# Moving one modulation block into attention, four products from GpSimd to VectorE, and a part of attention's modulation sums ahead of the gate products

## The chip, the cores and the metric

The kernel is one program on one core of a Trainium2 chip. The metric is the device time of one execution in microseconds (us). The engines are named as the profile names them: PE is TensorE's matmul, PEld its weight load, DVE is VectorE, ACT is ScalarE, POOL is GpSimd, SP is SyncE, whose queue issues the weight loads from HBM. Everything is float32.

## The reference

Two transformer blocks follow each other on 512 tokens of width 1024. What matters here, shortened:

```
mod = silu(c) @ w_ada + b_ada                    # 6 x 1024 numbers: shift, scale, gate of two branches
x = x + gate * rms_norm(mixer(rms_norm(x) * (1 + scale) + shift))      # mixer: two kinds of attention
x = x + gate * rms_norm(swiglu(...))
# second block: 9 x 1024 numbers from silu(c_2) @ w_mod_2 for x, and once more for 256 context tokens
x, xc = ffn with ffn_w_in_2[0], ffn_w_out_2[0]   # on x and on the context xc
x = x + gate * rms_norm(mLSTM and pooling mixer)
x = x + gate * rms_norm(swiglu(..., ffn_w_in_2[1], ffn_w_out_2[1]))
swiglu(h) = (silu(h @ w_gate) * (h @ w_up)) @ w_down        # 1024 -> 2816 -> 1024
```

## The kernel before

**Stages.** The first mixer (projections, selection, `attention`), then one block of code for the out-projection and two feed-forward layers (`stage_ffn_1_2`), the second mixer, and the last feed-forward layer.

**Attention** (line 1631) runs 48 pair steps; a step is a block of 128 queries with two heads. PE computes the scores of step i (L1706), turns the probabilities of step i - 2 (L1717) and multiplies those of step i - 3 with the values (L1734). Between them it takes 9, later 6 to 8 products of a `stream`: the feed-forward layer of the context tokens, which has nothing to do with attention. Its up part has tiles of 8 gate products (L874, bank 6) and 8 up products (L886, bank 7) up to step 23, its down part 8 outputs of 22 products (L913) from step 24 on. On DVE a step is two maxima (L1774), the normalisation of the step before (L1782, L1784 or L1788), and then `context_gate` (L952: waits for ACT's tanh of a finished gate tile, multiplies, frees bank 6) and `context_hidden` (L960, frees bank 7) of the tiles that fall due, and after them `some` instructions of modulation sums.

**Modulation.** The numbers of `mod` come in blocks of 512: a block's weights (2 MB, as two halves of 1 MB in `mod_half`) are multiplied by a vector and summed on DVE, eight sums (L1685, then seven L1687), a transpose (L699) and a reduction (L706), twice that with two vectors (for x and the context, blocks "mod" below 10). PE turns the result into columns with a small matmul (L776). `MODS_LATE` lists the jobs done in attention in order and `LATE_ENDS` the pair step by which each is due: a job begins in the step where the one before is due, and its instructions are spread evenly over its steps. Job j may begin when PE has turned job j - 2. The turning is placed at fixed tiles of the up part for jobs 0 to 5, ahead of down outputs 1, 3, 4, 5, 6 and 7 for jobs 6 to 11 (`more`), and at the end for 12 and 13. SP issues the half loads by `late(j, half)` (L1858), which waits until DVE has used up that half of the job before; between them stand the loads of the ring (L291), a ring of three buffers for all other weights, each of which waits until PE has left the buffer. `K.ring.load_ahead(sp, ("out1", 0))` loads half of w_out, 2 MB in three parts.

**The out-projection** (`out_tensor`, `out_scalar`, `out_vector`, lines 2150 to 2260) has 16 pieces of 8 products (L2144), for two halves of the tokens. ACT squares each piece (L1976) and scales it (L1977), DVE adds the squares (`y_add`, L1988), and after piece 8 PE sums them over the partitions (`y_sum`, L1997 and L1998). PE needs the addition of piece 6 and the square of piece 7 for it. Between the additions DVE does the update of the context tokens, coefficients, and two modulation blocks, 12 and 13 (`MODS_OUT`), whose ten instructions each (`side_sums`, L3088, seven of L3091, L3100, L3104) are taken by `spare(4)`, `spare(4)`, `spare(2)`, `spare(5)`, `spare(3)` and `spare(2)`. `spare(5)` stands after `coefs_2` and before the addition of piece 6. Their weights are loaded by `side_loads_out`.

**The three feed-forward layers** (calls 0, 1, 2 of `fast_tensor`, `fast_gpsimd`, `fast_scalar`, `fast_vector`) multiply in blocks with seven products in place of eight: POOL forms sums of weight blocks (four L2898 to L2903 for an up tile, L2911 and L2913, then L2973 and L2977, for a down output), DVE forms sums of token blocks and adds up the results. The up part has 22 tiles: four by themselves, then 8 pairs in a form of their own (`pair_tensor`, L2414), then two more by themselves (u = 4 = LEAD and u = 5). The products of a tile are named by lines: L2717, L2767, L2773, L2781, L2725, L2791, L2796; L2767 waits for POOL's L2900. A pair ends on POOL with `pair_products`: two products of Silu and up (L2662, 128x512 each) and a subtraction (L2666). A single tile ends there with L2945, L2947 and L2950. DVE makes `xs`, sums of the hidden blocks, for the down part: five L3074 after the last pair, L3261 for the tile u = 4, and L3209 for the last. The down part begins with L2839 (22 products with block b11), then L2847, which needs all of `xs`. In DVE's stream of a tile, L3166, L3233 and L3218 read the first results, L3267 gives block 21 and L3282 block 12, which ACT turns by Silu (L3040); ACT's L3038 is the Silu of block 11. In call 1 PE has 16 more products (L2806, the context's norm) ahead of L2839.

Of the kernel before, what the change touches and what calls it, by code (L numbers as in the profile page):

```python
# [9 lines left out]
ALU = mybir.AluOpType  # L10
# [72 lines left out]
def column_order():  # L83
# [5 lines left out]
    def plain(name):  # L89
# [16 lines left out]
HALF = SEQ // 2  # L106
MODS_START = 4
MODS_FIRST = 6
MODS_LATE = (("ada", 6), ("mod", 6), ("ada", 7), ("mod", 7), ("ada", 8), ("mod", 8), ("ada", 4), ("mod", 9), ("ada", 9),
             ("mod", 10), ("ada", 10), ("mod", 11), ("ada", 11), ("ada", 5))  # L110
LATE_ENDS = (4, 8, 11, 16, 18, 23, 27, 33, 36, 39, 41, 44, 46, 48)
MODS_OUT = (12, 13)
MODS_DOWN = {0: (14, 15), 1: (16, 17), 2: ()}
MODS_BOTH = 10
# [1516 lines left out]
def attention(K, M):  # L1631
# [64 lines left out]
    with nc.Block() as block:  # L1696

        @block.tensor
        def _(pe):
# [36 lines left out]
                last.then_inc(pv, 1)  # L1736

            columns = {f: {part: MODS_LATE[j]} for j, (f, part) in enumerate(((11, 0), (14, 1), (15, 0), (18, 1), (19, 0), (21, 1)))}
            more = {d: MODS_LATE[6 + j] for j, d in enumerate((1, 3, 4, 5, 6, 7))}
            stream = itertools.chain(  # L1740
                itertools.chain.from_iterable(context_up(
                    K, X, pe, f, columns.get(f, ()), (1,) if f == CTX_SCORER else (0, 1)) for f in ups),
# [15 lines left out]
                if i >= 3:  # L1758
                    values(i - 3)
            pe.wait_ge(X.y, KT)  # L1760
            modulation_columns(K, pe, MODS_LATE[12])
            modulation_columns(K, pe, MODS_LATE[13])

        @block.vector
        def _(dve):
# [26 lines left out]
            for i in range(len(pairs) + 1):  # L1792
                for half in range(2):
                    if i < len(pairs):
                        maximum(i, half)
                for half in range(2):
                    if i >= 1:
                        normalise(i - 1, half)
                for f in due(gate_slot, i):
                    context_gate(K, X, dve, f)  # L1800
                for f in due(up_slot, i):
                    context_hidden(K, X, dve, f)
                if i == LATE_ENDS[job] and job + 1 < len(MODS_LATE):
                    job += 1
                    left, steps = late_length(job), late_steps(dve, job)
                some = -(-left // max(LATE_ENDS[job] - i, 1))
                left -= some
                for _ in itertools.islice(steps, some):
                    pass

        @block.scalar
# [38 lines left out]
        def _(sp):  # L1850
# [32 lines left out]
            late(7, 1)  # L1883
            K.ring.load_ahead(sp, ("ctx_down", 3))
            late(8, 0)
            K.ring.load_ahead(sp, ("ctx_down", 4))
            late(8, 1)
            late(9, 0)
            K.ring.load_ahead(sp, ("ctx_down", 5))
            late(9, 1)  # L1890
            late(10, 0)
            K.ring.load_ahead(sp, ("ctx_down", 6))
            late(10, 1)
            late(11, 0)
            late(11, 1)
            K.ring.load_ahead(sp, ("ctx_down", 7))
            late(12, 0)
            late(12, 1)
            K.ring.load_ahead(sp, ("out1", 0))
            late(13, 0)  # L1900
            late(13, 1)
            K.ring.load_ahead(sp)
            sp.wait_ge(X.down, KT)
            sp.dma_start(K.x[:, :, CTX:TOK], K.spill).then_inc(K.restored, 16)
# [216 lines left out]
def out_fields(K, name, call, W, gain, scale, shift, banks, begun=0, context=False):  # L2121

    O = out_products(Fields(), name, banks, begun)
    O.context = context
    O.mm = Tally(K.out_mm, call * len(OUT_PIECES))
    flat = W.hid[:, :, :, :].rearrange("p a f n -> p (a f n)")
    y = flat[:, 0:KT * SEQ].rearrange("p (k n) -> p k n", k=KT)
    O.T = Tail(K, lambda k0, k1, a, b: y[:, k0:k1, a:b], OUT_PIECES, gain, W.squares, scale, shift,
               left=(2, 6))
    if context:  # L2130
        O.sq, O.sums, O.log, O.rstd_done, O.scaled, O.done = (K.sem(f"po_{n}") for n in (
            "sq", "sums", "log", "rstd", "scaled", "coefs"))
        O.total, O.rstd = K.ps[4][:, 0:CTX], W.side[:, 0:CTX]
        side_fields(K, O, W, MODS_OUT, 0)
        O.squares, O.z = ([W.side[:, CTX * i:CTX * i + CTX] for i in at] for at in ((1, 2), (3, 4)))
    return O

# [12 lines left out]
def out_tensor(K, O, pe):  # L2150

    for i in range(len(OUT_PIECES)):
        if i >= 3:
            O.T.s["scaled"].wait(pe, i - 2)
        out_piece(K, O, pe, i, range(4) if i < O.begun else range(KT), True).then_inc(O.mm.sem, 1)
        if i in (KT + 3, 2 * KT - 1):
            K.ring.left(O.mm.sem, O.mm.base + i + 1)
        if O.context and i < 4:
            for k in (2 * i, 2 * i + 1):
                pe.wait_ge(O.sq, k + 1)  # L2160
                pe.matmul(O.total, K.ones[:, :], O.squares[k % 2], start=(k == 0),
                          stop=(k == KT - 1)).then_inc(O.sums, 1)
        if O.context and i in (KT + 2, KT + 6):
            modulation_columns(K, pe, ("mod", O.side[0 if i == KT + 2 else 1]))
        if i == KT:
            y_sum(K, O.T, pe, 0)
        if i == KT + 4:
            x_sum(K, O.T, pe, 0)
# [133 lines left out]
def fast_fields(K, call, W, prev, gain, scale=None, shift=None, context=False, by_rows=None):  # L2302
# [13 lines left out]
    F.side = MODS_DOWN[call]  # L2316
    F.coefs = K.sem(f"coefs{call}") if F.side else None
    if F.side:
        side_fields(K, F, W, F.side, len(MODS_OUT) + sum(len(MODS_DOWN[c]) for c in range(call)))
    F.in_down = False  # L2320
    F.T = Tail(K, lambda k0, k1, a, b: K.h[:, k0:k1, CTX + a:CTX + b], FFN_PIECES, gain, W.squares, scale, shift,
               left=(2, 2) if context else (6, 6))
# [36 lines left out]
def pair_fields(K, F, scr, base):  # L2359
# [2 lines left out]
    counts = (96, 96, 96, 96, 96, 96, 48, 32) + (24, 24, 27, 1) + (8, 4, 4, 4, 8, 8)  # L2362
    n = len(F.pairs)
    done = dict(args=13, t=3 * n, s=3 * n, d1=n, d2=n, begun=2 * n, y_kept=2 * n, w=3 * n, f=3 * n, c=2 * n, full=n, rows=3 * n,
                diff=3 * n, cols=6 * n, silu=2 * n, hid=n, token=4, formed=n)
    F.R = {name: Tally(sem, count + done[name] * K.pair_calls) for name, sem, count in zip(PAIR_SEMS, spent, counts)}
    K.pair_calls += 1
    W = F.W
# [288 lines left out]
def pair_products(K, F, pool, e):  # L2657

    R, f = F.R, 2 * F.pairs[e]
    for n, (half, buf) in enumerate(((1, F.c_buf[e % 2]), (0, F.F_buf[e % 2]))):  # L2660
        R["silu"].wait(pool, 2 * e + n + 1)
        ins = pool.tensor_tensor(pair_hidden(F, e, half), buf[:, 0:2], buf[:, 2:4], ALU.mult)  # L2662
        if n == 0 and f + 1 >= FH:
            K.pool.link(pool, ins)
            j0, j1 = max(f, FH) - FH, f + 2 - FH
            pool.tensor_tensor(F.b12[:, j0:j1], F.b22[:, j0:j1], F.b12[:, j0:j1], ALU.subtract)  # L2666
    ins.then_inc(R["hid"].sem, 1)

# [30 lines left out]
def fast_tensor(K, F, pe):  # L2701
# [110 lines left out]
    for d in range(4):  # L2812
# [18 lines left out]

        if d == 0 and F.pairs:
            F.R["hid"].wait(pe, len(F.pairs))
            S["hid"].wait(pe, LEAD)
        else:
            S["hid"].wait(pe, FH if d == 0 else F.ups)
# [49 lines left out]
def fast_gpsimd(K, F, pool):  # L2886
# [47 lines left out]
        F.R["d2"].wait(pool, n)  # L2934
        up_weight_sums(LEAD + 1)

    for u, f in enumerate(F.tiles):
        j = f % FH
        one, two = (F.b11, F.b12) if f < FH else (F.b21, F.b22)
        if F.pairs and u == LEAD - 1:  # L2940
# [190 lines left out]
def side_loads_out(K, O, sp):  # L3131

    side_load(K, O, sp, 0, 0)
    side_load(K, O, sp, 0, 1)
    sp.wait_ge(*O.side_half[0])
    side_load(K, O, sp, 1, 0)
    sp.wait_ge(*O.side_full[0])
    side_load(K, O, sp, 1, 1)


def side_loads(K, F, sp):
# [27 lines left out]
def fast_vector(K, F, dve):  # L3169
# [19 lines left out]
    for u in range(F.units):  # L3189
# [50 lines left out]
        if u < F.units - 1:  # L3240
            give_22()
        if F.pairs and u == LEAD:
            F.R["hid"].wait(dve, len(F.pairs))
            steps = pair_hidden_sums(F, dve)
        if F.pairs and u == LEAD - 1:
            pair_rows(K, F, dve, 0, (0, 1))
# [19 lines left out]
        S["c21"].wait(dve, u + 1)  # L3266
        dve.tensor_tensor(out21, pc, F.v, ALU.add).then_inc(S["got21"].sem, 1)  # L3267
        spare(2)
        if F.ups <= u < F.units - 1:
            S["xsum"].wait(dve, x_count(d) + 4)  # L3270
            for a, b in HALVES:
# [8 lines left out]
            pair_rows(K, F, dve, 0, (2,))  # L3280
        S["c12"].wait(dve, u + 1)
        dve.tensor_tensor(out12, pb, F.v, ALU.add).then_inc(S["got12"].sem, 1)  # L3282
        spare(2)


# [852 lines left out]
```

## Time and profile before

| what | us |
|---|---|
| median of 3 runs | 2096.37 |
| the runs | 2096.37, 2096.44, 2093.59 |
| the profiled execution | 2093.89 |
| its span, first to last instruction | 2092.0 |
| PE busy | 2060.4 (98%) |
| DVE busy | 1509.1 (72%) |
| POOL busy | 837.2 (40%) |
| ACT busy | 535.2 (26%) |

The views are of that one profiled execution. Busy PE is not PE at its peak, since matmuls are pipelined and their ends are modelled. Times in the timelines are from the start of the span.

### The profile page before, as it was taken

The numbers are of one execution on the slowest core, as the hardware profiler recorded it, in microseconds if no ns is written. First come the engines' busy times: TensorE is split into PE (matmuls) and PEld (weight loads), VectorE is DVE, ScalarE is ACT, GpSimd is POOL, SyncE is SP. The second block draws the span as 40 slices with busy tenths as digits, with TensorE's granted clock in tenths as the row PEclk, the third lists the DMA queues.
The fourth block names the chain that finished last, engine by engine and source line by source line (L and its number), as shares of the span: only waits on it lengthen the run. The fifth ranks groups of instructions, "written<-read, shape, count | busy, mean of one in ns | idle before, by whom it ended". The sixth has DMA issues, their size and how long they took to land. (4 is left out here: it accounts for less than half of the span.)

```text
span 2092.0 us, 25946 instructions
## 1 busy us (share of the span) xinstructions
PE 2060.4 (98%) x9775; PEld 1655.9 (79%) x9775; DVE 1509.1 (72%) x2423; ACT 535.2 (26%) x1260; POOL 837.2 (40%) x607
## 2 busy tenths in 40 slices
PE   9999999999999999999999999999999999999998
PEld 5446777777888888888888888888656888888887
DVE  6997978888568888756688886754726468888645
ACT  3443433344332111101401111103243431121101
POOL 0100200000104888845277876630011127787742
PEclk9999999999999999999999999999999999999999
DMA  9752566556632223343223224431122132232331
GB/s 377 251 188 74 159 222 205 180 164 195 226 117 75 89 81 107 91 130 96 81 81 113 90 68 124 124 109 51 57 110 81 54 104 85 85 117 56 83 83 41
DMA packets 244703, 252.28 MB, mean 121 GB/s; under 512 B 10154, under 2 KB 194916, under 8 KB 244324
## 3 DMA queue, kind: packets, MB, share of 16 engines
q1 hardware_dynamic: 243696, 249.17, 37.5%
q10 hardware_dynamic: 884, 1.46, 0.3%
q8 instruction: 79, 1.29, 0.3%
q14 instruction: 44, 0.36, 0.1%
HBM read 245.12 MB, written 4.21 MB: 119 GB/s over the span
## 5 line engine op out<-in xcount | busy, mean ns | idle before, releaser
L2898 POOL TENSOR_TENSOR w_sums<-ring 128x512 f32<-128x512 f32 x18 | 24.0, 1335 | 375.3 <-DMA ring<-in_w_gate_up 293.5
L2637 POOL TENSOR_TENSOR w_sums<-ring 128x256 f32<-128x256 f32 x144 | 135.0, 966 | 17.5 <-PE ps L2414 17.5
L2414 PE MATMUL ps<-pair_args,ring 128*128 128x256 f32 x576 | 136.1, 379 | 0.0
L2414 PE MATMUL ps<-h_sums,ring 128*128 128x256 f32 x576 | 132.2, 379 | 0.0
L2653 POOL TENSOR_TENSOR w_sums<-w_sums,ring 128x512 f32<-128x512 f32 x96 | 130.2, 1377 | 2.1
L2414 PEld LDWEIGHTS ps<-pair_args,ring 128*128 128x128 f32 x576 | 109.4, 190 | 14.9
L2414 PEld LDWEIGHTS ps<-h_sums,ring 128*128 128x128 f32 x576 | 109.1, 190 | 14.7
L2414 PE MATMUL ps<-h_sums,w_sums 128*128 128x256 f32 x480 | 115.3, 379 | 0.0
L2144 PE MATMUL ps<-h_act,ring 128*128 128x256 f32 x512 | 114.2, 381 | 1.0 <-PEq L1696 0.7
L2414 PE MATMUL ps<-h_act,w_sums 128*128 128x256 f32 x480 | 111.4, 379 | 0.0
L2144 PEld LDWEIGHTS ps<-h_act,ring 128*128 128x128 f32 x512 | 97.4, 191 | 14.5 <-issue 1.4
L1085 PE MATMUL ps<-h_act,ring 128*128 128x512 f32 (+1 forms) x240 | 104.2, 593 | 0.0
L2516 DVE TENSOR_TENSOR w_sums<-w_sums,ring 128x1024 f32<-128x1024 f32 x48 | 100.0, 2083 | 1.6
L2414 PEld LDWEIGHTS ps<-h_act,w_sums 128*128 128x128 f32 x480 | 91.2, 190 | 12.4
L2414 PEld LDWEIGHTS ps<-h_sums,w_sums 128*128 128x128 f32 x480 | 91.2, 190 | 12.4
L2911 POOL TENSOR_TENSOR w_sums<-ring 128x768 f32<-128x768 f32 (+1 forms) x24 | 41.4, 1726 | 129.8 <-DMA ring<-in_ffn_w_out 84.9
L886 PE MATMUL ps<-h_act,ring 128*128 128x256 f32 x352 | 88.3, 387 | 0.5 <-ACT rstd L933 0.5
L1085 PEld LDWEIGHTS ps<-h_act,ring 128*128 128x128 f32 (+1 forms) x240 | 44.8, 189 | 54.8 <-issue 54.3
L874 PE MATMUL ps<-h_act,ring 128*128 128x256 f32 x352 | 86.4, 385 | 0.7 <-ACT x_res L925 0.6
L2653 POOL TENSOR_TENSOR w_sums<-ring 128x512 f32<-128x512 f32 x48 | 65.7, 1389 | 45.5 <-PE ps L2414 30.3
L3267 DVE TENSOR_TENSOR h_act<-ps,rstd 128x256 f32<-128x256 f32 x30 | 12.6, 421 | 96.1 <-PE ps L2865 91.4
L1687 DVE SCALAR_TENSOR_TENSOR rstd<-mod_half,cc,rstd 128x512 f32<-128x512 f32 x98 | 73.5, 750 | 5.1 <-DMA mod_half<-in_w_ada 2.1
(593 smaller groups left out, 4909.7 us busy)
## 6 DMA issues: line engine op xcount, KB each, us to landing
ring<-in_ffn_w_in SPq DMA_DIRECT2D x66, 1024.0 KB, 7.6
ring<-in_w_gate_up SPq DMA_DIRECT2D x22, 1024.0 KB, 7.0
ring<-in_ffn_w_out SPq DMA_DIRECT2D x32, 704.0 KB, 6.5
mod_half<-in_w_ada SPq DMA_DIRECT2D x16, 1024.0 KB, 7.3
ring<-in_w_in SPq DMA_DIRECT2D x6, 2048.0 KB, 9.6
mod_half<-in_w_mod SPq DMA_DIRECT2D x12, 1024.0 KB, 5.2
pair_args<-in_w_mod SPq DMA_DIRECT2D x12, 1024.0 KB, 5.9
ring<-in_ffn_w_out SPq DMA_DIRECT2D x8, 1408.0 KB, 7.1
```

The lines of the kernel that those rows point to most:

```text
L874: last = pe.matmul(K.ps[6][:, 0:CTX], w[:, k, 0, a:a + P], K.h[:, k, 0:CTX], start=(k == 0), stop=(k == KT - 1))
L886: last = pe.matmul(K.ps[7][:, CTX:2 * CTX], w[:, k, 1, a:a + P], K.h[:, k, 0:CTX], start=(k == 0), stop=(k == KT - 1))
L1085: last = pe.matmul(bank(i)[0:rows, :], lhs(w, item, j, k), hl(k), start=(k == 0), stop=(k == KT - 1))
L1687: ins = dve.scalar_tensor_tensor(acc, M.mod[:, half, kk, :], c, acc, ALU.mult, ALU.add)
L2144: ins = pe.matmul(K.ps[O.banks[i]][:, 0:b - a], w[:, k, (d % 4) * P:(d % 4) * P + P], K.h[:, k, CTX + a:CTX + b], start=(k == O.first(i)), ...
L2414: last = pe.matmul(bank[:, HALF * at:HALF * at + HALF], weights[:, k], tokens[:, k], start=(begins and k == 0), stop=(k == 1), skip_group_ ...
L2516: dve.tensor_tensor(rows, rows if n else w[:, 0], w[:, n + 1], ALU.add).then_inc(R["rows"].sem, 1)
L2637: last = pool.tensor_tensor(F.diff[:, r, at], w[:, 2 * j:2 * j + 2, i], w[:, 2 * i:2 * i + 2, j], ALU.subtract)
L2653: pool.tensor_tensor(F.cols[:, k], F.cols[:, k] if n else w[:, k, 0], w[:, k, n + 1], ALU.add).then_inc(R["cols"].sem, 1)
L2898: pool.tensor_tensor(s1, a21, a22, ALU.add).then_inc(S["wsum"].sem, 1)
L2911: pool.tensor_tensor(s1[:, a:b], a21[:, a:b], a22[:, a:b], ALU.add).then_inc(S["wsum"].sem, 1)
L3267: dve.tensor_tensor(out21, pc, F.v, ALU.add).then_inc(S["got21"].sem, 1)
```

## The change

Block "mod" 12 becomes the last of now 15 jobs in attention, with new due steps; `more` gives a job to each of the down outputs 1 to 7, jobs 13 and 14 are turned at the end, and the loads of SP are put in a new order. The out-projection keeps block 13 alone. In a pair step of attention, the first half of the modulation instructions stands before `context_gate` and `context_hidden`, the second half after them. In each of the three feed-forward layers the last pair's second product (`pair_last_product`) and the three products of the last tile are done by DVE; POOL keeps the last pair's first product and the subtraction, and ends its loop one tile sooner.

```diff
-MODS_LATE = (("ada", 6), ("mod", 6), ("ada", 7), ("mod", 7), ("ada", 8), ("mod", 8), ("ada", 4), ("mod", 9), ("ada", 9),
-             ("mod", 10), ("ada", 10), ("mod", 11), ("ada", 11), ("ada", 5))
-LATE_ENDS = (4, 8, 11, 16, 18, 23, 27, 33, 36, 39, 41, 44, 46, 48)
+MODS_LATE = (("ada", 6), ("mod", 6), ("ada", 7), ("mod", 7), ("ada", 8), ("mod", 8), ("ada", 4), ("ada", 9), ("mod", 9),
+             ("ada", 10), ("mod", 10), ("ada", 11), ("mod", 11), ("ada", 5), ("mod", 12))
+LATE_ENDS = (4, 8, 11, 16, 18, 23, 27, 30, 34, 37, 40, 43, 45, 47, 49)
@@ attention, PE
-            more = {d: MODS_LATE[6 + j] for j, d in enumerate((1, 3, 4, 5, 6, 7))}
+            more = {d: MODS_LATE[5 + d] for d in range(1, KT)}
@@ attention, DVE
-                for f in due(gate_slot, i):
-                    context_gate(K, X, dve, f)
-                for f in due(up_slot, i):
-                    context_hidden(K, X, dve, f)
...
-                for _ in itertools.islice(steps, some):
+                for _ in itertools.islice(steps, some // 2):
+                    pass
+                for f in due(gate_slot, i):
+                    context_gate(K, X, dve, f)
+                for f in due(up_slot, i):
+                    context_hidden(K, X, dve, f)
+                for _ in itertools.islice(steps, some - some // 2):
                     pass
@@ attention, SP, the loads from job 8 on as they stand after the change
             late(8, 0)
             late(8, 1)
             K.ring.load_ahead(sp, ("ctx_down", 4))
             late(9, 0)
             late(9, 1)
             K.ring.load_ahead(sp, ("ctx_down", 5))
             late(10, 0)
             late(10, 1)
             late(11, 0)
             K.ring.load_ahead(sp, ("ctx_down", 6))
             late(11, 1)
             late(12, 0)
             K.ring.load_ahead(sp, ("ctx_down", 7))
             late(12, 1)
             late(13, 0)
             K.ring.load_ahead(sp, ("out1", 0))
             late(13, 1)
             late(14, 0)
             late(14, 1)
             K.ring.load_ahead(sp)
@@ out-projection
-        side_fields(K, O, W, MODS_OUT, 0)
+        side_fields(K, O, W, MODS_OUT[1:], 0)
-        if O.context and i in (KT + 2, KT + 6):
-            modulation_columns(K, pe, ("mod", O.side[0 if i == KT + 2 else 1]))
+        if O.context and i == KT + 2:
+            modulation_columns(K, pe, ("mod", O.side[0]))
@@ side_loads_out
-    sp.wait_ge(*O.side_half[0])
-    side_load(K, O, sp, 1, 0)
-    sp.wait_ge(*O.side_full[0])
-    side_load(K, O, sp, 1, 1)
@@ pair_products
-    for n, (half, buf) in enumerate(((1, F.c_buf[e % 2]), (0, F.F_buf[e % 2]))):
+    halves = ((1, F.c_buf[e % 2]), (0, F.F_buf[e % 2]))
+    for n, (half, buf) in enumerate(halves[0:1] if e == len(F.pairs) - 1 else halves):
...
+def pair_last_product(K, F, dve):
+
+    R, e = F.R, len(F.pairs) - 1
+    buf = F.F_buf[e % 2]
+    R["silu"].wait(dve, 2 * e + 2)
+    dve.tensor_tensor(pair_hidden(F, e, 0), buf[:, 0:2], buf[:, 2:4], ALU.mult).then_inc(R["formed"].sem, 1)
@@ fast_tensor, before the down part
             F.R["hid"].wait(pe, len(F.pairs))
+            F.R["formed"].wait(pe, len(F.pairs) + 1)
@@ fast_gpsimd
-    for u, f in enumerate(F.tiles):
+    for u, f in enumerate(F.tiles[0:-1]):
@@ fast_vector
         if F.pairs and u == LEAD:
+            pair_last_product(K, F, dve)
             F.R["hid"].wait(dve, len(F.pairs))
+            F.R["formed"].wait(dve, len(F.pairs) + 1)
             steps = pair_hidden_sums(F, dve)
...
         dve.tensor_tensor(out21, pc, F.v, ALU.add).then_inc(S["got21"].sem, 1)
         spare(2)
+        if u == F.ups - 1:
+            S["got21"].wait(dve, u + 1)
+            S["got11"].wait(dve, u + 1)
+            dve.tensor_tensor(b21[:, FH - 1], F.gate1[u % 2], out21, ALU.mult)
...
         dve.tensor_tensor(out12, pb, F.v, ALU.add).then_inc(S["got12"].sem, 1)
+        if u == F.ups - 1:
+            S["silu2"].wait(dve, u + 1)
+            S["got22"].wait(dve, u + 1)
+            K.dve.link(dve, dve.tensor_tensor(b22[:, FH - 1], out12, out22, ALU.mult))
+            dve.tensor_tensor(b12[:, FH - 1], b22[:, FH - 1], b12[:, FH - 1], ALU.subtract).then_inc(S["hid"].sem, 1)
         spare(2)
```

## Rows read from the trace of the kernel before

**Rows 1.** The page, busy time of each engine over the span.
```profile
PE 2060.4 (98%) x9775; PEld 1655.9 (79%) x9775; DVE 1509.1 (72%) x2423; ACT 535.2 (26%) x1260; POOL 837.2 (40%) x607
```
**Rows 2.** The waits of PE: us in total, times, longest.
```profile
PE ps L2847 <- DVE h_sums L3209: 3.9, 2, 1.9
PE ps L1997 <- DVE tmp L1988: 2.9, 1, 2.9
PE ps L2767 <- POOL w_sums L2900: 1.9, 3, 0.6
```
**Rows 3.** Busy time by stretch: PE, PEld, DVE, ACT, POOL, clock, DMA share, GB/s.
```profile
410.00:450.00 40.00, 40.00 (x273) 29.34 (x272) 32.34 (x87) 17.57 (x55) 0.00 (x0) 1.00 0.56 172
```
**Rows 4.** Timeline of PE in the out-projection: start, duration, instructions, idle before.
```profile
571.87 17.43 PE L2144 MATMUL ps<-h_act,ring 128*128 128x256 f32 x80
592.24 1.21 PE L1997 MATMUL ps<-tmp,ones 128*128 128x256 f32 x2 [2.93 <-DVE tmp L1988]
```
**Rows 5.** Timeline of PE, end of call 2's up part.
```profile
1944.41 4.91 PE L2839 MATMUL ps<-hidden,ring 128*128 128x256 f32 x22
1951.27 4.99 PE L2847 MATMUL ps<-h_sums,w_sums 128*128 128x256 f32 x22 [1.95 <-DVE h_sums L3209]
```
**Rows 6.** Stretches behind three waits of PE: busy, granted clock, DMA share, GB/s.
```profile
592.20:596.00 3.80, 3.77 (x10) 0.55 0.00 0
885.10:889.30 4.20, 4.18 (x12) 0.59 1.16 320
1951.20:1955.40 4.20, 4.13 (x19) 1.00 0.00 0
```
**Rows 7.** Timeline of DVE in the out-projection, before the column sum.
```profile
588.66 3.18 DVE L3091 SCALAR_TENSOR_TENSOR pair_args<-pair_args,cc 128x512 f32<-128x512 f32 x4
591.76 0.42 DVE L1988 TENSOR_TENSOR tmp<-tmp,sq 128x256 f32<-128x256 f32 x1
```
**Rows 8.** Timeline of DVE in attention, steps 45 to 47.
```profile
524.27 2.32 DVE L1687 SCALAR_TENSOR_TENSOR rstd<-mod_half,cc,rstd 128x512 f32<-128x512 f32 x3
526.63 0.71 DVE L699 STREAM_TRANSPOSE rstd<-rstd 128x512 f32<-128x512 f32 x1
...
536.55 0.49 DVE L1685 TENSOR_SCALAR rstd<-mod_half,cc 128x512 f32<-128x512 f32 x1 [5.36 <-PE ps L776]
```
**Rows 9.** Timeline of PE, end of attention.
```profile
553.26 0.62 PE L776 MATMUL ps<-mod_folded,cst 128*128 128x16 f32 x4
```
**Rows 10.** Timeline of SP in attention, the loads it issues.
```profile
516.95 2.00 SPq L291 DMA_DIRECT2D ring<-in_w_out  x3
520.89 6.10 SPq L1858 DMA_DIRECT2D mod_half<-in_w_ada  x2
```
**Rows 11.** Line L1858 from 500 to 540: issue to landing.
```profile
DMA to landing us min/median/max: 5.2/7.4/10.7
```
**Rows 12.** Timeline of PE, the scores of attention's step 47.
```profile
534.13 1.13 PE L1706 MATMUL ps<-dsa_k,dq_t 64*128 64x512 f32 x4
```
**Rows 13.** Timelines of DVE and PE around attention's step 7.
```profile
311.60 0.42 DVE L952 SCALAR_TENSOR_TENSOR x_res<-x_res,ps 128x256 f32<-128x256 f32 x1 [0.59 <-ACT x_res L946]
...
313.06 1.13 PE L874 MATMUL ps<-h_act,ring 128*128 128x256 f32 x4
```
**Rows 14.** Timeline of POOL, end of call 2's up part.
```profile
1929.72 1.27 POOL L2662 TENSOR_TENSOR hidden<-h_act 128x512 f32<-128x512 f32 x1
...
1946.87 0.73 POOL L2945 TENSOR_TENSOR hidden<-rstd,h_act 128x256 f32<-128x256 f32 x1
...
1949.04 3.48 POOL L2973 TENSOR_TENSOR ring<-ring 128x768 f32<-128x768 f32 x2
```
**Rows 15.** Timeline of DVE, end of call 2's up part.
```profile
1942.88 0.42 DVE L3267 TENSOR_TENSOR h_act<-ps,rstd 128x256 f32<-128x256 f32 x1 [0.77 <-PE ps L2791]
...
1949.11 2.01 DVE L3209 TENSOR_TENSOR h_sums<-hidden 128x256 f32<-128x256 f32 x1 [4.08 <-POOL hidden L2950]
1951.22 5.93 DVE L3213 TENSOR_TENSOR h_sums<-hidden,h_sums 128x1536 f32<-128x1536 f32 x2
```

More of the change, by code:

```diff
@@ L1760, in _ @@
             pe.wait_ge(X.y, KT)
-            modulation_columns(K, pe, MODS_LATE[12])
             modulation_columns(K, pe, MODS_LATE[13])
+            modulation_columns(K, pe, MODS_LATE[14])
         @block.vector
@@ L1885, in _ @@
             late(8, 0)
+            late(8, 1)
             K.ring.load_ahead(sp, ("ctx_down", 4))
-            late(8, 1)
             late(9, 0)
+            late(9, 1)
             K.ring.load_ahead(sp, ("ctx_down", 5))
-            late(9, 1)
             late(10, 0)
-            K.ring.load_ahead(sp, ("ctx_down", 6))
             late(10, 1)
             late(11, 0)
+            K.ring.load_ahead(sp, ("ctx_down", 6))
             late(11, 1)
+            late(12, 0)
             K.ring.load_ahead(sp, ("ctx_down", 7))
-            late(12, 0)
             late(12, 1)
+            late(13, 0)
             K.ring.load_ahead(sp, ("out1", 0))
-            late(13, 0)
             late(13, 1)
+            late(14, 0)
+            late(14, 1)
             K.ring.load_ahead(sp)
@@ L2318, in fast_fields @@
     if F.side:
-        side_fields(K, F, W, F.side, len(MODS_OUT) + sum(len(MODS_DOWN[c]) for c in range(call)))
+        side_fields(K, F, W, F.side, len(MODS_OUT[1:]) + sum(len(MODS_DOWN[c]) for c in range(call)))
     F.in_down = False
@@ L2364, in pair_fields @@
     done = dict(args=13, t=3 * n, s=3 * n, d1=n, d2=n, begun=2 * n, y_kept=2 * n, w=3 * n, f=3 * n, c=2 * n, full=n, rows=3 * n,
-                diff=3 * n, cols=6 * n, silu=2 * n, hid=n, token=4, formed=n)
+                diff=3 * n, cols=6 * n, silu=2 * n, hid=n, token=4, formed=n + 1)
     F.R = {name: Tally(sem, count + done[name] * K.pair_calls) for name, sem, count in zip(PAIR_SEMS, spent, counts)}
@@ L2665, in pair_products @@
             j0, j1 = max(f, FH) - FH, f + 2 - FH
-            pool.tensor_tensor(F.b12[:, j0:j1], F.b22[:, j0:j1], F.b12[:, j0:j1], ALU.subtract)
+            ins_12 = pool.tensor_tensor(F.b12[:, j0:j1], F.b22[:, j0:j1], F.b12[:, j0:j1], ALU.subtract)
+            if e == len(F.pairs) - 1:
+                ins = ins_12
     ins.then_inc(R["hid"].sem, 1)
+def pair_last_product(K, F, dve):
[3 more added lines that the diff above has]
+    dve.tensor_tensor(pair_hidden(F, e, 0), buf[:, 0:2], buf[:, 2:4], ALU.mult).then_inc(R["formed"].sem, 1)
 def up_sums(F, f):
```

## The prediction

> **What bounds the kernel now.** I read the page's busy times first, then who waited for whom on TensorE, then the timelines of all engines around the longest of those waits. TensorE is busy for 2060.4 of 2092.0 us [rows 1], so an edit pays only where TensorE stands still, or runs at its lower clock. Its waits are few and short [rows 2], and they name three places that the diff touches. One is the wait of the first output projection's column sum for DVE (2.9 us, once). One is the wait of the down product L2847 for the DVE addition L3209 (3.9 us in 2 places). One is the wait of L2767 for POOL's weight sums (1.9 us in 3 places). In attention TensorE has practically none: busy 40.00 of 40.00 us in the window shown, with DVE at 32.34 [rows 3].
>
> A wait costs a little more than its idle time. In call 2, L2839's 22 products start at 1944.41; at 0.216 us each (80 in 17.43 us, the last 0.38 long [rows 4]) the next could start at 1949.16, and starts at 1951.27 [rows 5]: 2.1 us for 1.95 shown. Two waits also cost clock. After the one at 592.24 the granted clock averages 0.55 over 3.8 us, that is, mostly the 1.2 GHz level: 0.45 x 3.8 = 1.7 us lost. After the one at 885.12 it averages 0.59 over 4.2 us, again 1.7 us. After the twin at 1951.27 it stays 1.00 [rows 6]. So a wait of this length may or may not cost a clock drop.
>
> **Part 1, modulation block 12 leaves the out-projection for attention.** DVE's in-order stream there ends with the second block: one L3088 and four L3091 (3.18 us from 588.66) stand before the addition L1988 at 591.76 [rows 7]. TensorE had all it needed at 571.87 + 80 x 0.216 = 589.15 and waited to 592.24 [rows 4]: 3.1 us. With one block only, its ten steps are used up by the first three spare calls, so L1988 (0.42) follows the coefficients at about 588.1 and ends at about 588.6, before 589.15. Its other input, ScalarE's square of piece 7, was long there. So the 3.1 us go, and with them the 1.7 us of clock: 4.8 us. What is late next is only the chain through the x update, and it shifts with its sum. The two side loads that go freed nobody; the two small column products go from here to attention, 0.3 us each way.
>
> In attention DVE gets ten more instructions: eight sums of 0.48 to 0.75, a transpose of 0.71 and a reduction that I take as long [rows 8], 7.1 us in all. I cost them at nothing because DVE has about 8 us free per 40 [rows 3] and because it stood 5.36 us at L1685 waiting for TensorE's columns two jobs back [rows 8]. The new due steps remove that wait: the last job starts at step 47, when block 11's columns are turned at the head of that step. Job 14's last five instructions (3 x 0.75 and 2 x 0.71) follow the last normalisation, which ends at 546.5 or so: 550.3. TensorE turns the last columns at 553.26, behind its own work [rows 9]. If that cover were gone, each late microsecond would be one of TensorE.
>
> The queue order needs a look. In the new list the second half of job 13 is issued directly behind the 2 MB of w_out that went out at 516.95, and its first half before. Before, the first half stood in that place, issued at 520.89 [rows 10], and landed 10.7 us later, the longest landing of this line [rows 11], at 531.6. I take the same landing for the second half. DVE reaches the fifth sum of step 45 near 527.5, so it stands some 4 us. Behind it are the sum (0.75) and both maxima of step 46 (1.3), which end at 533.7. TensorE wants them for the scores of step 47, at 534.13 [rows 12]. The margin is 0.4 us. Bounds: a gain of 0.2 us (the little wait at 543 that the 5.36 us caused goes), a loss of 2 us if the load lands 2 us later. I take 0.
>
> **Part 2, half of a pair step's sums before the gate products.** It adds nothing; it delays L952 by at most two sums of 0.75, less the time for which DVE stood before L952 anyway. The tightest case of 14 is step 7: L952 starts at 311.60 after 0.59 us idle, and the next gate product starts at 313.06 [rows 13]. With 1.46 us of sums inserted it ends near 312.9. So at most 0.1 us is lost there; of the other tiles none has less room. DVE spends its waits for ScalarE's tanh on sums. But TensorE does not wait for DVE here, so 0.
>
> **Part 3, the last pair's second product goes to DVE.** POOL's second L2662 (from 1929.72, 1.27 us) goes [rows 14], and with it everything POOL does behind it comes 1.2 us earlier. DVE's new product falls between and takes POOL's way for some 0.5 us, so I take 0.7. L2767 waits for POOL's L2900, 0.65 us in each of three calls [rows 2], 0.8 with the restart, so 0.7 x 3 = 2.1 us. Bounds 0.3 and 0.8 each.
>
> **Part 4, the last tile's three products go to DVE.** POOL did L2945, L2947 and L2950 only from 1946.87, behind four weight sums; then came DVE's L3209, and then TensorE [rows 5, 14]. On DVE they follow L3267 and L3282 [rows 15] plus ScalarE's Silu. How long does a product of two buffers take on DVE? L3267, which reads PSUM and one buffer, takes 0.42 us with POOL busy. L3209, which reads two buffers, takes 2.01: it starts 0.07 us after POOL's L2973 and ends 0.3 us after that one's end [rows 14, 15]. Then DVE and POOL alternate, two L3213 in 5.93 us. So each new DVE product waits out the POOL instruction in progress.
>
> The Trainium skill states this in "SBUF — State Buffer", Who interferes with whom: a DVE instruction with two SBUF inputs and a GpSimd one that reads SBUF exclude each other, and the first issued blocks the other to its end. By that rule every one of the four products could wait a full POOL instruction; the trace's L3209 agrees.
>
> Placing them, shifted by the 0.7 us of part 3: gate product from 1942.7, waits to 1943.2, ends 1943.6. L3282 ends 1944.3, Silu 1944.8; second product ends 1945.4. Subtraction waits for POOL until 1946.9, ends 1947.2 (POOL's instructions are about 1.5 and 1.75 us long). L3209 waits for L2973 until 1949.0, ends 1949.3. TensorE starts L2847 at 1949.45, and could from 1948.47: a wait of 1.0 us instead of 2.1. Bounds: uncontended (0.42 each) it is 0; with one more POOL instruction in the way, it is 2.1 as now. So 1.1 us in each of calls 0 and 2, bounds 0 and 2.1. In call 1 two column sums cover it, so nothing. With half the wait left, I take the clock drop of call 0 as gone too: 1.7 us.
>
> **Sum.** 4.8 + 0 + 2.1 + 2 x 1.1 + 1.7 = 10.8 us. The profiled execution took 2093.89 us (span 2092.0, so 1.9 around it): 2083.1. It is 2.5 us faster than the median of the runs shown, 2096.37; two are at 2096.4, one at 2093.6, perhaps one or two clock drops apart. If those fall at waits that go, the median comes down to 2083; if elsewhere, 2085.6. I say 2083.8.
>
> **Rivals.**
> A. DVE and POOL get in each other's way at the end of the up phase, and parts 3 and 4 bring only the 2.1 us or less. For it: the 2.01 us of L3209. Against: two of the four products start in times when POOL's instruction is nearly over. It gives 4.8 + 2.1 = 6.9: 2087.0, and up to 2089.5 on the median. The Trainium skill says of moves between these two engines ("Perfetto Trace Analysis", Optimizing Scalar/DVE Operations) that they might not help; this is that case.
> B. The products slip through: waits at L2847 gone. 10.8 + 2 x 1.0 = 12.8: 2081.1.
> C. Attention: the half load behind w_out lands late. DVE then holds the maxima, TensorE the scores of step 47. It decides from a landing of 532.0. Slower than before it ends only if the landing is past 543, over 11 us late (less 1.7 if the clock falls). The three last jobs have two steps each, five instructions a step, and leave DVE little to catch up with. Priced at 15.5 us of stall, a landing near 547.5: 2098.6. Against: the same place in the queue landed at 531.6.
> D. The removed out-projection wait is only exchanged, as ScalarE or the x read back are next. Against: the piece at 589.15 has both inputs. It gives 10.8 - 4.8 = 6: 2088.
>
> **Chances.** Forecast 0.55, A 0.18, B 0.13, C 0.02 for a slower end and 0.05 for a loss of 2 to 6 us (2085 to 2089), D 0.05, no effect that can be measured 0.02. The range for 8 in 10 holds forecast, B and most of A: 2080.0 to 2089.5. A measurement of this kernel tells some 0.2%, 4.2 us, from no change. Faster by more: all but the worse part of C, D and A, 0.93; within 0.05; slower 0.02.
>
> **What would show it.** Right: no wait of L1997 for L1988, clock 1.00 around 590; L2767's wait under 0.3 us; L2847's wait about 1 us, ended by L3209; the DVE products of the last tile at up to 2 us each; one DVE wait of 3 to 5 us for the load of mod_half near 528. Wrong: waits of the scores L1706 or of L886 in attention, a wait for the new product's semaphore at L2839, or L2847 waiting 2 us.

## The result, and the profile after

The changed kernel takes 2085.49 us in the median of four runs (2082.39 to 2087.41), the kernel before 2096.4 (2093.59 to 2096.93, four runs): a ratio of 0.9949, 95% interval 0.9932 to 0.9966, 10.9 us faster. The forecast was 2083.8, the sum of its steps 10.8 us, the range 2080.0 to 2089.5.

The total is right, and in part by luck. A loss that the steps do not have stands against gains that they have too small, and the kernel before took longer than usual in these four runs: in its 56 runs beside the experiments its median is 2093.67, while the changed kernel's nine runs in all have 2086.56, which is 7.1 us less.

Medians, differences and ratios go by fast runs; one run of the kernel before, of 6495 us, is left out of them. The profiled execution took 2084.14 us, with a span of 2082.3 (2092.0 before).

The page of the changed kernel, busy time of each engine over the span:

```profile
PE 2057.6 (99%) x9775; PEld 1654.3 (79%) x9775; DVE 1522.7 (73%) x2435; ACT 536.5 (26%) x1260; POOL 827.6 (40%) x595
```

Twelve more instructions on DVE, twelve fewer on POOL; PE is busy 2.8 us less [rows 1]. A clock drop, a short stretch at the lower level of the granted clock, costs 1.7 us; ahead of its last 2 us the kernel before has two of them in its profiled execution and the changed one has one, which makes 1.7 of the 2.8 us. The rest isn't placed. Where the time went shows in the start of the same PE instruction in both timelines:

| instruction | before | after | after less before |
|---|---|---|---|
| first scores after the block boundary at 272 | 272.56 | 272.12 | -0.44 |
| first product of the out-projection | 554.53 | 556.04 | +1.51 |
| its column sum (L1997, now L2001) | 592.24 | 590.65 | -1.59 |
| call 0, L2847 (now L2863) | 885.12 | 879.10 | -6.02 |
| call 1, L2717 (now L2732) | 1023.78 | 1016.08 | -7.70 |
| second mixer, L1997 (now L2001) | 1421.90 | 1413.29 | -8.61 |
| last feed-forward layer's entry, L3714 (now L3737) | 1557.95 | 1551.00 | -6.95 |
| call 2, L2847 (now L2863) | 1951.27 | 1941.87 | -9.40 |

Every stage but two gains. Attention is 1.95 us longer, and the second mixer 1.7. The waits of PE in the changed kernel (us in total, times, longest) name the first:

```profile
PE ps L874 <- DVE x_res L952: 2.1, 1, 2.1
PE ps L2889 <- DVE h_act L3230: 1.6, 3, 0.5
...
PE ps L2863 <- DVE h_sums L3221: 0.8, 2, 0.4
```

The waits of [rows 2] for L1988 and for L2900 are gone, that for L3209 (now L3221) is 0.8 instead of 3.9. At the top stands one that the kernel before has not: a gate product of the context's layer waits for L952. The timeline of all engines shows how it comes about (start, duration, instructions, idle before and what ended it):

```profile
272.08 0.93 SPq L1860 DMA_DIRECT2D mod_half<-in_w_ada  x2
...
277.40 0.48 DVE L1685 TENSOR_SCALAR rstd<-mod_half,cc 128x512 f32<-128x512 f32 x1 [4.27 <-DMA mod_half<-in_w_ada]
277.80 0.41 DVE L952 SCALAR_TENSOR_TENSOR x_res<-x_res,ps 128x256 f32<-128x256 f32 x1
...
278.36 0.67 PE L874 MATMUL ps<-h_act,ring 128*128 128x256 f32 x2 [2.09 <-DVE x_res L952]
```

The same place in the kernel before:

```profile
275.00 0.42 DVE L952 SCALAR_TENSOR_TENSOR x_res<-x_res,ps 128x256 f32<-128x256 f32 x1 [1.43 <-ACT x_res L946]
...
277.93 0.49 DVE L1685 TENSOR_SCALAR rstd<-mod_half,cc 128x512 f32<-128x512 f32 x1 [0.77 <-DMA mod_half<-in_w_ada]
```

In step 0 the first modulation job has three instructions to give, `some // 2` is one, and that one is the first sum of the first half load, issued at the start of attention. DVE has waited for this load before too, but behind L952; now L952, which frees bank 6, stands behind the wait. PE loses 2.47 us from start to start where 0.22 would do: 2.25 us.

The out-projection went as forecast. Timeline of PE in the changed kernel:

```profile
573.38 17.43 PE L2148 MATMUL ps<-h_act,ring 128*128 128x256 f32 x80
590.65 0.59 PE L2001 MATMUL ps<-tmp,ones 128*128 128x256 f32 x2
```

Timeline of DVE in the same stretch:

```profile
588.21 1.51 DVE L789 TENSOR_TENSOR mod<-ps,par 32x32 f32<-32x32 f32 x8
...
589.99 0.42 DVE L1992 TENSOR_TENSOR tmp<-tmp,sq 128x256 f32<-128x256 f32 x1
```

No wait, against 2.93 us in [rows 4]. DVE's addition ends at 590.41 and PE wants it at 590.66: it is no more than 0.25 us early.

The end of the up phase of call 2 in the changed kernel, timeline of DVE:

```profile
1935.03 0.42 DVE L3281 TENSOR_TENSOR h_act<-ps,rstd 128x256 f32<-128x256 f32 x1 [0.78 <-PE ps L2806]
1935.49 0.71 DVE L3286 TENSOR_TENSOR hidden<-rstd,h_act 128x256 f32<-128x256 f32 x1
1936.76 0.42 DVE L3300 TENSOR_TENSOR h_act<-ps,rstd 128x256 f32<-128x256 f32 x1 [0.56 <-PE ps L2811]
1937.66 0.43 DVE L3304 TENSOR_TENSOR hidden<-h_act 128x256 f32<-128x256 f32 x1 [0.48 <-ACT h_act L3056]
1938.12 1.65 DVE L3305 TENSOR_TENSOR hidden<-hidden 128x256 f32<-128x256 f32 x1
1939.80 1.92 DVE L3221 TENSOR_TENSOR h_sums<-hidden 128x256 f32<-128x256 f32 x1
```

Timeline of POOL there:

```profile
1934.04 1.87 POOL L2929 TENSOR_TENSOR w_sums<-w_sums,ring 128x768 f32<-128x768 f32 x1
...
1937.67 1.81 POOL L2929 TENSOR_TENSOR w_sums<-w_sums,ring 128x640 f32<-128x640 f32 x1
1939.45 3.67 POOL L2989 TENSOR_TENSOR ring<-ring 128x768 f32<-128x768 f32 x2
```

Timeline of PE there:

```profile
1936.56 4.91 PE L2855 MATMUL ps<-hidden,ring 128*128 128x256 f32 x22
1941.87 4.99 PE L2863 MATMUL ps<-h_sums,w_sums 128*128 128x256 f32 x22 [0.40 <-DVE h_sums L3221]
```

These answer to [rows 5, 14, 15]. The new product L3286 (0.71 us) begins in the last 0.42 us of POOL's first L2929 and ends 0.29 us after it. The product L3304 (0.43 us) begins 0.01 us ahead of POOL's next L2929. The subtraction L3305 begins 0.45 us behind the start of that L2929 and also ends 0.29 us after it; L3221 begins 0.35 us behind L2989. DVE's sums are ready 5.16 us after L2855 starts, and PE wants them after 4.75.

The granted clock (columns: busy time of PE, PEld, DVE, ACT, POOL, then the clock, DMA share, GB/s), in the stretches of [rows 6] and in one of the second mixer:

```profile
588.60:592.40 3.80, 3.80 (x20) 3.33 (x19) 1.69 (x10) 1.40 (x4) 0.00 (x0) 1.00 0.00 0
879.00:883.20 4.20, 4.10 (x19) 3.66 (x20) 4.14 (x2) 1.41 (x2) 4.20 (x2) 1.00 1.10 368
1941.80:1946.00 4.20, 4.13 (x19) 3.70 (x20) 4.18 (x2) 1.37 (x2) 4.20 (x2) 1.00 0.39 95
1534.30:1538.30 4.00, 4.00 (x8) 1.87 (x8) 0.37 (x2) 0.75 (x2) 0.03 (x1) 0.57 1.02 384
```

Both drops behind waits [rows 6] are gone. A new one, 0.43 x 4.0 = 1.7 us, stands at 1534, where no wait is and the diff changes nothing: it is the second mixer's 1.7 us in the table.

### The profile page after: what moved, and what is told of

Same layout as the page of the kernel before. It is cut to its first block and busy times, and to the rows that moved or that the text cites. A ratio compares the mean times of both kernels' runs of the same rounds, so it can differ in the third digit from the quotient of the medians.

```text
span 2082.3 us, 25952 instructions
## 1 busy us (share of the span) xinstructions
PE 2057.6 (99%) x9775; PEld 1654.3 (79%) x9775; DVE 1522.7 (73%) x2435; ACT 536.5 (26%) x1260; POOL 827.6 (40%) x595
## 5 line engine op out<-in xcount | busy, mean ns | idle before, releaser
L874 PE MATMUL ps<-h_act,ring 128*128 128x256 f32 x352 | 86.4, 386 | 2.8 <-DVE x_res L952 2.1
L886 PE MATMUL ps<-h_act,ring 128*128 128x256 f32 x352 | 88.3, 387 | 0.5 <-ACT rstd L933 0.5
L1687 DVE SCALAR_TENSOR_TENSOR rstd<-mod_half,cc,rstd 128x512 f32<-128x512 f32 x105 | 78.6, 749 | 7.2 <-DMA mod_half<-in_w_ada 4.5
```

The source lines that it names most:

```text
L874: last = pe.matmul(K.ps[6][:, 0:CTX], w[:, k, 0, a:a + P], K.h[:, k, 0:CTX], start=(k == 0), stop=(k == KT - 1))
L886: last = pe.matmul(K.ps[7][:, CTX:2 * CTX], w[:, k, 1, a:a + P], K.h[:, k, 0:CTX], start=(k == 0), stop=(k == KT - 1))
L1687: ins = dve.scalar_tensor_tensor(acc, M.mod[:, half, kk, :], c, acc, ALU.mult, ALU.add)
```

## The experiments

Each is timed in five rounds beside the kernel before, on one chip for each group; e1 to e4 are a group, e5 to e8, then e9 with e10, and e11. The kernel before had medians of 2094.41, 2093.76, 2093.14 and 2093.68 in them (the expectations give the first as 2094.6). "Less" is the difference from the median of the same group.

| run | median (fastest) | less | ratio, 95% interval |
|---|---|---|---|
| e1 changed, no split | 2081.72 (2080.24) | 12.7 | 0.9938, 0.9926 to 0.9951 |
| e2 before, split alone | 2098.03 (2096.08) | -3.6 | 1.0019, 1.0010 to 1.0028 |
| e3 changed, no split in step 0 | 2080.48 (2080.06) | 13.9 | 0.9936, 0.9924 to 0.9949 |
| e4 before, block 12 alone | 2089.95 (2086.63) | 4.5 | 0.9978, 0.9969 to 0.9987 |
| e5 before, last pair alone | 2090.88 (2089.27) | 2.9 | 0.9984, 0.9975 to 0.9993 |
| e6 before, last tile alone | 2088.70 (2086.35) | 5.1 | 0.9972, 0.9961 to 0.9982 |
| e7 e1, POOL waits | 2081.03 (2079.31) | 12.7 | 0.9934, 0.9921 to 0.9946 |
| e8 e3, all sums ahead | 2081.06 (2080.26) | 12.7 | 0.9939, 0.9927 to 0.9952 |
| e9 changed, split in step 0 alone | 2088.33 (2084.65) | 4.8 | 0.9972, 0.9961 to 0.9984 |
| e10 e7, load first | 2080.39 (2079.01) | 12.8 | 0.9938, 0.9925 to 0.9952 |
| e11 the changed kernel again | 2086.56 (2083.98) | 7.1 | 0.9962, 0.9949 to 0.9976 |

**What the split costs.** e1 takes it away from the changed kernel, e2 puts it alone into the kernel before, e3 and e9 divide it between step 0 and all other steps.

```diff
@@ e1, with the three other moves; e2 is the same hunk the other way round, alone
-                for _ in itertools.islice(steps, some // 2):
-                    pass
...
-                for _ in itertools.islice(steps, some - some // 2):
+                for _ in itertools.islice(steps, some):
                     pass
@@ e3; e9 has `0 if i else some // 2`
-                for _ in itertools.islice(steps, some // 2):
+                ahead = some // 2 if i else 0
+                for _ in itertools.islice(steps, ahead):
                     pass
...
-                for _ in itertools.islice(steps, some - some // 2):
+                for _ in itertools.islice(steps, some - ahead):
```

> The changed kernel with all modulation sums of a pair step behind the gate products again (the other moves kept). Theory 1 (the split costs one wait, at the first gate tile of attention: DVE stands 4.3 us for the load of mod_half before its first sum, and L952 now stands behind that sum): the 2.09 us wait of L874 for L952 near 278 is gone, attention is 2.3 us shorter, 2083.2 in the median against 2085.5 for the changed kernel. Rival 2 (the split pays elsewhere what it costs there): no difference, 2085.5. Rival 3 (the wait near 278 comes from the new order of jobs and loads, not from the split): the wait stays, 2085.5.

> The kernel before with the split alone. Theory 1: one new wait of 2.1 us near 278 (start to start 2.47 instead of 0.22), all else as before, 2096.4 + 2.3 = 2098.7. Rival 2: the split gains back in steps 1 to 23, 2096.4 or less. Rival 3 (it is the job order): no wait near 278, 2096.4.

> The changed kernel with the split in every pair step but step 0, where all sums stand behind the gate products. Theory 1: the wait near 278 is gone and nothing else comes: as e1 within 0.3 us in its span, 2083.2. Rival (the sums ahead delay L952 of other tiles too, each below what the waits show): the span stays above that of e1 by 0.5 us or more. If instead the split in the other steps helps TensorE, the span is below that of e1.

> The changed kernel with the split in step 0 alone (one sum, L1685, ahead of the first L952), all other sums behind the gate products. Theory 1: that one instruction is the whole cost of the split, by the load it waits for: the 2.1 us wait near 278 is back, fastest run 2.2 us above e1's fastest (2080.2), 2082.4, and the median up to 1.7 us more where the clock drops behind that wait: 2083 to 2085.5. Rival (the split in the other steps takes part in it): below 2081.5 in the fastest run.

Without the split the wait near 278 is gone, with the split alone it is there, without it in step 0 it is gone, with step 0 alone it is there. The PE timeline of e2:

```profile
279.11 0.99 PE L874 MATMUL ps<-h_act,ring 128*128 128x256 f32 x2 [2.72 <-DVE x_res L952]
```

The PE timeline of e9:

```profile
278.83 0.67 PE L874 MATMUL ps<-h_act,ring 128*128 128x256 f32 x2 [1.99 <-DVE x_res L952]
```

So theory 1 holds, and neither the order of jobs (e2 has the old one) nor the later steps have a part: e3's runs at a mean clock of 1.000 have spans of 2078.3 to 2078.7, e1's 2078.4 and 2078.6. But the size expected was too small. e1 and e3 came out 1.5 and 2.7 us below their expectations, and e9's median lies 6.6 us above e1's (on another chip), not 1.3 to 3.8; e9's fastest run, forecast at 2082.4, took 2084.65. That led to the next run.

> The changed kernel once more, beside e9, whose median (2088.3) lies 3.4 us above where the theory put its worst case, though its fastest run (2084.65) shows a wait of 2.0 us and one clock drop behind it. Theory: the wait near 278 costs 2.2 us in every run and a clock drop of 1.7 us in some, and further drops come at places that have nothing to do with it; then runs of the changed kernel lie between 2082.4 and 2088, by their mean clock: 2082.4 at 1.000, 2084 at 0.999, 2086 to 2088 at 0.998 to 0.997. Rival (the split of the later steps helps, so that the changed kernel is faster than e9): fastest run 2082.4, median below 2084.

The changed kernel's nine runs in both sets lie between 2082.39 and 2089.49, and the slower ones have the lower mean clock (2082.39 and 2083.98 at 1.000, 2089.49 at 0.996). Two, 2088.42 and 2089.49, lie above the 2088 of the theory. The rival, a median below 2084, falls. e11's profiled execution was its slowest run, and shows the wait in another size. Its PE timeline:

```profile
280.64 1.19 PE L874 MATMUL ps<-h_act,ring 128*128 128x256 f32 x2 [3.69 <-DVE x_res L952]
```

Its DVE timeline:

```profile
279.68 0.49 DVE L1685 TENSOR_SCALAR rstd<-mod_half,cc 128x512 f32<-128x512 f32 x1 [5.87 <-DMA mod_half<-in_w_ada]
```

What its first two half loads took from issue to landing (L1860 from 271 to 276; the first is the shorter):

```profile
DMA to landing us min/median/max: 6.8/7.9/9.0
```

In the first execution of the changed kernel this load took 5.2 us. In the 13 profiles of this case it took 5.1 to 6.8, and each later microsecond is one of PE when L952 stands behind it: the four executions that have the wait had the load in 5.1, 5.2, 5.8 and 6.8 us, and PE idle for 1.99, 2.09, 2.72 and 3.69 us. The theory's 2.2 us in every run is therefore wrong; it is a wait of 2.0 to 3.7 us that follows the load. In three of these four executions the clock fell right behind it (e2, e9, e11), and in e11 for twice as long as in the two others, 0.50 x 6.85 = 3.4 us lost in place of 1.7 (the row of this stretch in e11, columns as above):

```profile
279.95:286.80 6.85, 6.16 (x16) 4.51 (x17) 4.38 (x14) 0.88 (x4) 0.00 (x0) 0.50 0.16 37
```

Over all runs the cost can be split in two. The 15 runs with a sum ahead in step 0 (the changed kernel's nine and e9's six) take 2086.7 us in the mean, the 15 runs of e1, e3 and e8, which differ from them only in where the sums stand, 2081.3. By the mean clocks of the runs, 4.7 and 1.9 us are lost to the lower clock. So of the 5.4 us some 2.6 are the wait itself and some 2.8 clock (an estimate, since the mean clocks are known to a thousandth, 2 us, for each run). Where the clock fell in the runs without a profile isn't known, nor whether all of these 2.8 us come from the wait.

**How far the sums may go ahead.** e8 is e3 with one line changed.

```diff
-                ahead = some // 2 if i else 0
+                ahead = some if i else 0
```

> As e3, but in every step after the first all modulation sums, not half of them, stand ahead of the gate products. In step 7 three more instructions of 0.7 us (2.1 us) go ahead of an L952 that ends 1.8 us before TensorE wants its bank: 0.3 us lost there, and steps with five sums ahead lose as much. So small waits of L874 for L952 and of L886 for L960 in several of 14 tiles, 1 to 3 us in all: 2081.5 to 2083.5 against e3's 2080.5. Rival (TensorE has slack in every tile whatever DVE does, the wait near 278 was the load alone): as e3, 2080.5.

No wait of L874 or L886 beyond those of before shows in attention, the time is e3's within the runs' scatter: the rival is right. PE has slack in every tile for all the sums that DVE does ahead, and only the wait for the first load is longer than the slack.

**Block 12 alone.** e4 takes the diff's part 1 into the kernel before: MODS_LATE and all that hangs on it, and no other hunk.

```diff
+LATE_ENDS = (4, 8, 11, 16, 18, 23, 27, 30, 34, 37, 40, 43, 45, 47, 49)
...
+        side_fields(K, O, W, MODS_OUT[1:], 0)
```

> The kernel before with modulation block 12 moved into attention alone (jobs, due steps, turning places, order of loads, and the out-projection with one block). As predicted: the 2.9 us wait of L1997 gone and the clock at 1.00 behind it, 4.8 us less than before, no new wait of TensorE in attention: 2091.6. Rival: attention pays for the ten more DVE instructions and the later load (DVE stands 4.5 us for it), 1 to 2 us, 2093.

4.5 us less in the median, and the column sum follows at once (PE timeline of e4):

```profile
571.41 17.43 PE L2146 MATMUL ps<-h_act,ring 128*128 128x256 f32 x80
588.67 0.59 PE L1999 MATMUL ps<-tmp,ones 128*128 128x256 f32 x2
```

Attention pays nothing that can be seen. DVE does stand for the late half load. The DVE timeline of the changed kernel, end of attention:

```profile
533.71 0.75 DVE L1687 SCALAR_TENSOR_TENSOR rstd<-mod_half,cc,rstd 128x512 f32<-128x512 f32 x1 [4.48 <-DMA mod_half<-in_w_ada]
```

e10 puts that load first, on top of e7, whose DVE waits 4.34 us there:

```profile
532.01 0.75 DVE L1687 SCALAR_TENSOR_TENSOR rstd<-mod_half,cc,rstd 128x512 f32<-128x512 f32 x1 [4.34 <-DMA mod_half<-in_w_ada]
```

> As e7, and the second half of job 13 is issued ahead of the 2 MB of w_out instead of behind it. Theory: DVE's 4.3 us wait for that load near 528 goes (issued at 519.7, landed 5 to 6 us later, wanted at 527.7), and TensorE does not see it, since in e7 it had no wait there either: time as e7, 2081.0 in the median. Rival (the late half cost something in attention's last steps, below what the waits show): 0.5 us or more less in the fastest run than e7's 2079.3.

```diff
-            K.ring.load_ahead(sp, ("out1", 0))
             late(13, 1)
+            K.ring.load_ahead(sp, ("out1", 0))
```

The DVE timeline of e10:

```profile
525.03 3.18 DVE L1687 SCALAR_TENSOR_TENSOR rstd<-mod_half,cc,rstd 128x512 f32<-128x512 f32 x4
```

The four sums run through. The wait of 4.3 us is gone, and the fastest run gains 0.3 us on e7's, less than the scatter: the wait was hidden, as the theory has it.

**The two DVE moves, each alone.** e5 is `pair_last_product` with its waits in the kernel before, e6 the three products of the last tile.

```diff
@@ e5
...
+            pair_last_product(K, F, dve)
...
@@ e6
+    for u, f in enumerate(F.tiles[0:-1]):
...
+            dve.tensor_tensor(b21[:, FH - 1], F.gate1[u % 2], out21, ALU.mult)
...
```

> The kernel before with the last pair's second product on DVE alone, in all three layers. Forecast step: L2767's wait for POOL's L2900 shrinks by 0.7 us in each of three calls; the changed kernel had it gone, 0.8 each, 2.4 in all. POOL is 1.2 us ahead of its old place behind it and TensorE only 0.8, so the wait of L2847 should shrink by 0.4 in calls 0 and 2 too: 3.2 us less than before (2094.6): 2091.4. Rival (POOL's last tile is held by TensorE's results, not by POOL's own queue): L2847's wait stays at 1.95, 2.4 us less: 2092.2.

> The kernel before with the three products of the last tile on DVE alone. L2767's waits stay. L2847's wait: the changed kernel shows 0.4 left of 1.95, with one new product clear of POOL's instructions (0.43 us) and one and L3209 in their way (1.65, 1.92). If where they fall is what sets the price, POOL's later place here (0.4 us against TensorE) changes it, 0 to 1.1 us left. 1.1 to 2 us less in two calls, and the clock drop behind call 0's wait gone (1.7): 3 to 5.5 us less than before (2094.6): 2089.1 to 2091.6. Rival (the products on DVE cost as much as on POOL once each waits out a POOL instruction): the wait stays near 1.9 and the time at 2094.6.

The waits of PE in e5:

```profile
PE ps L2859 <- DVE h_sums L3221: 3.9, 2, 2.0
```

The waits of PE in e6:

```profile
PE ps L2767 <- POOL w_sums L2900: 1.9, 3, 0.6
...
PE ps L2847 <- DVE h_sums L3209: 0.8, 2, 0.4
```

e5: L2767's wait is gone in all three calls, L2847's stays at 1.9: the rival's 2.4 us, measured 2.9. POOL did not get ahead of PE by the 0.4 us that the expectation counted. Its second product took 1.27 us [rows 14], but the subtraction before it takes 1.60 us beside DVE's new product (1.26 in the kernel before), so POOL gains 0.9 us, and PE 0.8. e6: the wait shrinks to 0.40 with part 3 or without, 5.1 us less in the median, inside the range expected. 2 x 1.55 and the clock drop of call 0 make 4.8. Not all of it need be e6's: the wait of L1997 in the out-projection, which e6 doesn't touch, is 1.83 us in its profile and 2.93 in that of the kernel before, so it differs between executions too.

e4, e5 and e6 together give 4.5 + 2.9 + 5.1 = 12.5 us, and e1, which has all three, 12.7: the moves add up.

**Who slows L3221.** e7 lets POOL's L2989 of the first down output wait for DVE's last addition.

```diff
+        else:
+            S["xsum"].wait(pool, FH)
         for a, b in HALVES:
             pool.tensor_tensor(a21[:, a:b], a11[:, a:b], a21[:, a:b], ALU.subtract).then_inc(S["wsum"].sem, 1)
```

> As e1 (the changed kernel without the split), and POOL's two L2989 of the first down output wait until DVE has added the last of xs (L3221). Theory: L3221 takes 1.9 us only because POOL's L2989 starts 0.35 us before it and shares the path to the buffers; alone it takes about 0.42. Then the 0.40 us wait of L2863 in calls 0 and 2 goes (0.56 us each with the restart), 1.1 us less than e1 (2081.7), 2080.6; POOL's weight sums start 0.8 us later, which nobody waits for, since TensorE wants them at 1946.7 and they are done at 1943.1. Rival (1.9 us is DVE's own time for this instruction, or POOL's next sums are on the path): no gain, or a new wait at L2869.

The DVE timeline of e7, call 2:

```profile
1937.61 0.43 DVE L3221 TENSOR_TENSOR h_sums<-hidden 128x256 f32<-128x256 f32 x1
```

Its POOL timeline:

```profile
1938.21 6.11 POOL L2989 TENSOR_TENSOR ring<-ring 128x768 f32<-128x768 f32 x2 [0.91 <-DVE h_sums L3221]
```

Its PE timeline:

```profile
1934.36 4.91 PE L2853 MATMUL ps<-hidden,ring 128*128 128x256 f32 x22
1939.11 4.91 PE L2861 MATMUL ps<-h_sums,w_sums 128*128 128x256 f32 x22
```

The same instruction takes 0.43 us instead of 1.92, and the wait of L2863 (L2861 in e7) is gone in both calls. The fastest run is 0.9 us below e1's, the median 0.7; the step was 1.1. POOL's two L2989 now take 6.11 us instead of 3.67, beside DVE's next two sums, and nobody waits for them. This is the rule of the Trainium skill, "SBUF — State Buffer", Who interferes with whom, that the prediction weighed: two inputs from the buffers on DVE and POOL's reads exclude each other, and 1.5 us of L3221 was that (1.92 less 0.43). e7 is also the version to keep: its slowest run, 2081.30, is faster than the fastest of the changed kernel's nine, 2082.39. e3 (2080.48), e10 (2080.39) and e1 (2081.72) can't be told from it.

## Why the prediction was right, step by step

- **Part 1, 4.8 us: right.** The wait and its clock drop are gone; e4 alone measures 4.5. DVE stands 4.48 us for job 13's second half up to 533.7, forecast "some 4 us" near 528, and the scores of step 47 come at 536.25 in a kernel that is 2 us later there: no stall. Job 14 ends at 551.7, forecast 550.3. The addition before the column sum came 0.3 us later against PE than forecast and still in time.
- **Part 2, 0: this step failed, by a wait that it put at nothing.** "The tightest case of 14 is step 7; of the other tiles none has less room" looked at the sums as work of 0.75 us each, and for work it holds: even with all sums ahead nothing is lost (e8). It did not ask what the first inserted instruction waits for. In step 0 that is the load that has only just been issued, and the row of the kernel before says so, idle of DVE and all: 0.77 us for the load at 277.93, 2.9 us after L952. It costs 2.25 us in the profiled execution, and 2.0 to 3.7 us of idle PE with, in three of four such executions, a clock drop behind it. In medians that makes more: 3.6 us in e2's median.
- **Part 3, 0.7 x 3: right in kind, slightly small.** The waits went altogether, 0.8 each with the restart, which was the upper bound.
- **Part 4, 1.1 in each of two calls: the size was off.** L2863 waits 0.40 us, start to start 0.56 more than without, instead of 2.11: 1.55 in each call. The rule that a product waits out the POOL instruction in progress held for three of four (L3286, L3305 and L3221); the fourth, L3304, was ahead of POOL by 0.01 us and took 0.43. What the instructions cost hangs on how much of POOL's instruction is left: 0.71, 1.65 and 1.92 us. The last sum is ready 5.16 us after L2855's start; the placement, in PE's own time, had 5.59.
- **Clock, 2 x 1.7: both drops gone.** In exchange one came at 1534 in the profiled execution, in a place untouched. The forecast allowed 0.7 us in all for what the median has above the sum; drops in untouched places take more.

Put together for the profiled pair: 4.8 + 2.4 + 3.1 + 1.7 = 12.0 from the moves, less 2.25 at step 0 and 1.7 at 1534, is 8.1. The span is 9.7 shorter. Of the other 1.6 us, 0.4 lie ahead of attention, 0.5 in two waits at its end (the little one near 543, 0.25 us, went, and the entry of the out-projection waits 0.4 instead of 0.7 us), and 0.3 behind the table's last row; the rest is spread.

Of the rivals, B's mechanism is true of one product of four (L3304 slips through), A's is seen at two instructions (L3305 and L3221) and does not eat up the gain, C and D did not come: C looked at the loads of attention, but at the last ones, where it was the first.

## What to carry to other kernels

When work is moved ahead of something in an in-order stream, ask of its first instruction what it waits for, not only how long it takes: a wait that cost nothing behind a release costs, ahead of it, all that exceeds the slack (here DVE waited 4.27 us and PE lost 2.25). Such a step is safe where its data has long been there, and is left out of the one step where it hasn't, at the start of the stage. And a sum that comes out right is no proof of its steps: here the moves gained 12.7 us without the split (e1) where 10.8 were forecast, the split took back 5.4 us in the mean, and the kernel before stood 2.7 us higher in the four runs of the result than in its other 56.

## What the runs showed of the hardware

Here a wait of PE of 1.8 us or more is followed by a clock drop in some executions only: of 16 such waits in the 13 profiles, 8. Their length doesn't decide: 2.93 and 1.93 us were followed by one, 2.91, 2.09 and 1.95 not. One drop costs 1.7 us; the one behind the longest wait, 3.69 us, cost 3.4. Drops also come with no such wait near, at 225 and 1532 to 1540, in some executions of several kernels, behind or among small matmuls (64x31 and 4x4 in shape); what decides there stays open. In every profile the clock is low once more in the last 0.9 to 4.4 us. A load of 1 MB issued at the same point of the program lands after 5.1 to 6.8 us, and where PE waits for it, its idle time differs by as much, 1.99 to 3.69 us.
